# Two-block transformer kernel: order of the opening DMAs and of head 0's projections, and gate columns on GpSimd

## The reference, cut to what matters

```python
mod = silu(c) @ ada_w0 + ada_b0              # c: 1024, ada_w0: 1024 x 3072
shift, scale, gate = split(mod, 3)
h = rmsnorm(x, norm_g0) * (1 + scale) + shift
q, k, v, z = split(h @ w_in0, 4)             # w_in0: 1024 x 4096
q, k = rope(q), rope(k)                      # 8 heads, 2 components of 64 each
p = softmax(q0 k0) - lam * softmax(q1 k1)    # per head
o = rmsnorm(p @ v) * silu(z)
x = x + gate * (o @ w_out0)
```

## Time and profile before

| | us |
|---|---|
| median of 3 runs | 3085.14 |
| lowest and highest of them | 3079.88, 3085.21 |
| the profiled execution | 3082.07 |
| its span in the trace | 3080.3 |

### The profile page before, as it was taken

The page is one execution under the profiler, slowest core; times in us unless marked ns, Lnnn a source line. Parts: engine busy times, 40 slices in busy tenths (PEclk is TensorE's granted clock), DMA queues, the critical chain, the costliest instruction groups (busy, mean ns, idle before and its releaser), DMA issues.

```text
span 3080.3 us, 34996 instructions
## 1 busy us (share of the span) xinstructions
PE 2777.5 (90%) x13113; PEld 2176.5 (71%) x13113; DVE 1675.0 (54%) x2177; ACT 1307.7 (42%) x1842; POOL 0.2 (0%) x4
## 2 busy tenths in 40 slices
PE   4899999997889988898987789998689999999996
PEld 2677777775667766676766567666567878888775
DVE  5688888887453055555554635554644434334344
ACT  4567666665224133333332435565424313223232
POOL 0000000000000000000000000000000000000000
PEclk7999999998889999999999889999799999999998
DMA  7211111110211111121221310000211111111111
GB/s 257 98 39 43 48 48 44 45 34 27 89 34 45 50 56 47 50 67 49 67 61 41 106 41 21 28 15 14 82 41 41 44 51 46 50 48 40 49 42 68
DMA packets 215821, 166.96 MB, mean 54 GB/s; under 512 B 9562, under 2 KB 203058, under 8 KB 215730
## 3 DMA queue, kind: packets, MB, share of 16 engines
q1 hardware_dynamic: 215530, 165.68, 17.3%
q10 hardware_dynamic: 200, 0.06, 0.0%
HBM read 153.14 MB, written 12.58 MB: 54 GB/s over the span
## 4 chain that ended last, share of the span: by engine, by line
PE 79%; DVE 8%; ACT 5%; DVEq 2%; issue 2%; SPq 1%; DMA 1%; ACTq 0%
PE PS L516 19%; PE PS L518 18%; PE PS L517 18%; PE PS L1012 4%; PE PS L1666 3%; PE PS L985 2%; PE PS L999 2%; PE PS L989 1%; PE PS L1621 1%; PE PS L1656 1%; PE PS L2155 1%; PE PS L2168 1%; DVEq L1808 1%; PE PS L2179 1%; DVE rest L507 1%
## 5 line engine op out<-in xcount | busy, mean ns | idle before, releaser
L516 PE MATMUL PS<-h_high,w_high 128*128 128x512 f32 x2144 | 858.8, 401 | 59.8 <-DVE h_low L583 18.9
L517 PE MATMUL PS<-h_low,w_high 128*128 128x512 f32 x2144 | 844.7, 394 | 0.0
L518 PE MATMUL PS<-h_high,w_low 128*128 128x512 f32 x2144 | 844.6, 394 | 0.0
L516 PEld LDWEIGHTS PS<-h_high,w_high 128*128 128x128 f32 x2144 | 408.7, 191 | 159.6 <-issue 62.7
L518 PEld LDWEIGHTS PS<-h_high,w_low 128*128 128x128 f32 x2144 | 407.7, 190 | 87.1
L517 PEld LDWEIGHTS PS<-h_low,w_high 128*128 128x128 f32 x2144 | 408.8, 191 | 81.8 <-issue 0.5
L538 DVE TENSOR_TENSOR w_low<-raw_weights,w_high 128x1024 fp32r<-128x1024 f32 (+2 forms) x159 | 182.9, 1155 | 216.3 <-ACT w_high L533 215.5
L533 ACT ACTIVATE w_high<-raw_weights 128x1024 fp32r<-128x1024 f32 (+2 forms) x159 | 158.6, 1001 | 243.8 <-PE PS L518 233.1
L765 DVE SCALAR_TENSOR_TENSOR residual<-PS,rest,residual 128x512 f32 (+1 forms) x112 | 83.3, 750 | 244.2 <-PE PS L518 240.5
L1088 ACT ACTIVATE residual<-PS,rest 128x1024 f32<-128x1024 f32 x128 | 141.4, 1110 | 174.3 <-DVE rest L1217 174.3
L2717 DVE SCALAR_TENSOR_TENSOR gated<-rest,gated 128x1024 f32<-128x1024 f32 x44 | 56.6, 1286 | 255.0 <-ACT gated L2686 255.0
(11 more groups left out here) (307 smaller groups left out, 3972.5 us busy)
## 6 DMA issues: line engine op xcount, KB each, us to landing
raw_weights<-in_w_in SPq DMA_DIRECT2D x59, 512.0 KB, 4.1
activations<-in_w_ada SPq DMA_DIRECT2D x16, 1536.0 KB, 7.0
raw_weights<-in_w_up SPq DMA_DIRECT2D x44, 512.0 KB, 3.9
raw_weights<-in_w_out SPq DMA_DIRECT2D x24, 512.0 KB, 4.1
rest<-in_ada_w SPq DMA_DIRECT2D x16, 576.0 KB, 4.9
activations<-in_ada_w SPq DMA_DIRECT2D x8, 1024.0 KB, 13.7
x_kept<-residual SPq DMA_DIRECT2D x2, 4096.0 KB, 13.3
residual<-x_kept SPq DMA_DIRECT2D x2, 4096.0 KB, 13.5
```

What stands on the lines that cost most here:

```text
L516: e.matmul(out_, wh[:, k, :], xh[:, k, cols], start=first, stop=False)
L517: e.matmul(out_, wh[:, k, :], xl[:, k, cols], start=False, stop=False)
L518: return e.matmul(out_, wl[:, k, :], xh[:, k, cols], start=False, stop=last_k)
```

## The change

1. All nineteen vector pieces are sent from ScalarE's queue at the start; SyncE sends only the `lam` vectors after its large loads.
2. Head 0 projects queries and keys in phase A and z and values in phase B. `place` maps a chunk to its position and bank. ScalarE and VectorE do the queries and keys with their high and low parts first; z, values, head 1's first weight split and silu(z) follow.
3. The gate columns' products and sums move from VectorE to GpSimd, as 8 multiplications in place and 7 additions for each of two halves. It starts when norm 0 is done. TensorE's `mod_pe` for them comes behind chunks 6 and 7, and VectorE's `mod_out` between the low parts of queries and keys.
4. The second half of the shift: ScalarE's copy before tile 1 instead of tile 3, TensorE's columns behind the second contraction tile of phase A instead of ahead of it.

```diff
--- before.py
+++ after.py
@@ sync_small, sync_gates, scalar_loads
     def sync_small(e):
-        load_pieces(e, pieces[10:])
...
         for i in range(2):
-            e.dma_start(first_raw[i], w_cols("w_in0", (1 + i) * D, P)).then_inc(slot_full[2 + i], 16)
+            e.dma_start(first_raw[i], w_cols("w_in0", (3 - i) * D, P)).then_inc(slot_full[2 + i], 16)
...
     def scalar_loads(e):
-        load_pieces(e, pieces[:10])
+        load_pieces(e, pieces)
@@ tensor_setup
         shift_products(e, 1)
-        shift_columns(e, 1)
@@ the gate columns
-    def gate_products(e, i):
-        ada_products(e, 2 + i, gates[i], {0: (gate_ld[i], 48 if i else 16)})
+    def gpsimd_gates(e):
+
+        e.wait_ge(s["md_acc"], 2)
+        e.wait_ge(n0_ready[0], n0_ready[1] + NT)
+        for i in range(2):
+            x = gates[i]
+            e.wait_ge(gate_ld[i], 48 if i else 16)
+            for k in range(NT):
+                e.tensor_scalar(x[k], x[k], silu_c[:, k:k + 1], None, ALU.mult)
+            for k in range(1, NT):
+                e.drain()
+                last = e.tensor_tensor(x[0], x[0], x[k], ALU.add)
+            last.then_inc(s["md_acc"], 1)
@@ norm, scalar part
-                    if scalar_after is not None and t == 3:
+                    if scalar_after is not None and t == 1:
@@ diff_attention
+        FIRST_ORDER = [Q, Q + 1, Q + 2, Q + 3, 0, 1, V_AT, V_AT + 1]
+
+        def place(hh, c):
+
+            return FIRST_ORDER.index(c) if isinstance(hh, int) and hh == 0 else c
...
         def bank(hh, c):
-            return banks(c if isinstance(hh, int) and hh == 0 else PJ)
+            return banks(place(hh, c) if isinstance(hh, int) and hh == 0 else PJ)
...
         def sync(e):
             for i in range(2):
-                load_tile(e, 0, i)
+                e.dma_start(raw[i], w_cols("w_in0", COLUMNS[1 + i] * P, P)).then_inc(full[i], 16)
@@ pe_first
                     if k == NT - 1:
                         last.then_inc(pj, 1)
+                if k == 1:
+                    shift_columns(e, 1)
...
                 last.then_inc(pj, 1)
-                if c in (4, 6):
+                if c > 5:
                     e.wait_ge(pjA, 1)
-                    mod_pe(e, c // 2, 0, ada_acc, 4)
+                    mod_pe(e, c - 4, 0, gates[c - 6][0], 4)
@@ act_chunk
-            e.wait_ge(pj, 8 * hh + c + 1)
+            e.wait_ge(pj, 8 * hh + place(hh, c) + 1)
@@ diff_attention, scalar
-            for c in range(8):
+            for c in range(Q, V_AT):
                 act_chunk(e, 0, c)
-                if c == 5:
-                    act_split(e, 1, 0)
-            act_silu(e, 0)
 
             e.wait_ge(s["x_kept"], 16)
             act_query_high(e, 0, QUERIES)
             act_key_high(e, 0)
             act_key_copy(e, 0)
+            for c in (0, 1, V_AT, V_AT + 1):
+                act_chunk(e, 0, c)
+            act_split(e, 1, 0)
+            act_silu(e, 0)
@@ diff_attention, vector
-            for i in range(2):
-                gate_products(e, i)
-                for c in range(Q + 2 * i, Q + 2 * i + 2):
-                    dve_rope(e, 0, c)
-                mod_out(e, 2 + i, 16 + 4 * i, column["ada_b0"] + 16 + 4 * i, 0, 4)
-            dve_split(e, 1, 0)
+            for c in range(Q, V_AT):
+                dve_rope(e, 0, c)
             e.wait_ge(s["x_kept"], 16)
             dve_query_low(e, 0, QUERIES, 0)
+            for i in range(2):
+                mod_out(e, 2 + i, 16 + 4 * i, column["ada_b0"] + 16 + 4 * i, 0, 4)
             dve_key_low(e, 0)
+            dve_split(e, 1, 0)
@@ end of the program
+    @blk.gpsimd
+    def _(e):
+        gpsimd_gates(e)
```

## The result

The changed kernel is slower. Its median is 3101.04 us (3092.68 to 3103.08), beside 3085.14 us (3076.02 to 3087.78) for the kernel before on the same chip: ratio 1.0052, 95% interval 1.0038 to 1.0066. The forecast was 3075.4 us in a range of 3065 to 3088, so the time lies outside the range and the sign is the opposite of the one forecast. What came is rival 3, the slower side: GpSimd itself is slow at these instructions. The profiled execution took 3103.08 us with a span of 3101.3, 21.0 us above that of before.

What follows compares the result with a forecast made beforehand. TensorE (79% of the chain) was taken as the bound. Norm 0's end 86.0, GpSimd 29.8, contention 6.7 and 4.2 us put scores at 126.7, not 133.40: 3082.07 less 6.7 is 3075.4 us, range 3065 to 3088.

Steps and rivals of the forecast that it cites:

- rival 3: GpSimd itself slow at the gate sums: at 2.5 times VectorE's times, scores at 140.7 and 3089.4 us; chance 0.10.
- GpSimd alone, 29.8 us: Gate-column sums on GpSimd without contention: 14.9 us per half, 29.8 us for both, at 1.7 times VectorE's times.
- Norm 0's end, 86.0: Norm 0 was to end at 86.0 instead of 86.75, 0.7 us earlier; GpSimd's gate sums start then.
- Rival 4: Opening gives nothing, through held-up issues or `lam` vectors landing at 43: 3.9 us missing, time 3079.3 us; chance 0.05.
- The first term, 3.9 us from the opening: Opening: `lam` vectors land near 41.0, moving the lambda multiplication from 44.95 to 41.0, 3.9 us; bounds 2 to 5.
- The two new waits: Norm 0: high and low parts held behind the shift copies, 1.9 us, and VectorE waiting for `shift_columns`, 1.3 us.
- Phase A, first matmul at 66.8: TensorE ends `shift_products` at 66.8 and starts phase A then, instead of at 74.7.
- Contention, 6.7 us: VectorE's work beside GpSimd's gate sums delays their end by 6.7 us, the middle of bounds 0 and 13.5.
- From the last sum to the scores, 4.2 us: After GpSimd's last sum, `mod_pe`, `mod_out` and the key and last query low parts take 4.2 us before the scores.
- The claim that ScalarE and the queries are hidden: Before head 0's scores, query and key work and ScalarE's 7 us of later work cost nothing, covered by the gate-column wait.
- from 133.40 on all moves as one block: From head 0's first scores on, TensorE sets the pace and everything shifts together by the 6.7 us gained.
- rival 2: Only one of VectorE and GpSimd works at a time: 13.5 us added, scores at 133.5, 3082.2 us; chance 0.22.

Runs made afterwards that it cites:

- experiment 11: Changed kernel, but SyncE issues head 0's first weight columns only after the lambda product: 3096.04 us, ratio 1.0047 to the kernel before.
- 12: Kernel before with all vector pieces on ScalarE's queue and the first weight columns issued behind the lambda product: 3082.94 us, ratio 1.0005.
- experiment 1: Changed kernel with GpSimd's gate-column products and additions left out, so results are wrong: 3074.57 us, ratio 0.9974 to the kernel before.
- experiment 4: Changed kernel with GpSimd starting when its gate rows have landed, not after norm 0: 3075.74 us, ratio 0.9980 to the kernel before.
- experiment 6: Kernel before with all vector pieces and the four `lam` vectors sent from ScalarE's queue: 3063.99 us, ratio 0.9938.

## Why the prediction was wrong

It had the path right: the last `mod_pe` waits for GpSimd, `mod_out` waits for that, and the key low parts stand behind it. It had the sizes wrong. The scores were forecast at 126.7 and started at 144.82, 18.1 us later. By the prediction's own terms:

- **GpSimd alone, 29.8 us: +14.8.** This is the step that failed: the ratio of 1.7, taken from the memset, as the price of all of GpSimd's instructions. By the changed kernel's rows the undisturbed work is 16 multiplications of 1.56 us and 14 additions 1.40 us apart, 44.6 us. The ratio to VectorE's 17.5 us is 2.5, where I took 1.7 from a one-column memset, and the rival's condition for "slower" was 2.09. The ratio isn't even one number: 3.2 for the multiplication (1.56 / 0.49), 1.9 for the addition (1.28 / 0.69). At 1.7 the addition had been put at 1.17 us, not far off, but the multiplication at 0.83, half of what it took: 11.6 of the 14.8 us are the multiplications'. The memset writes one column and says nothing of the rate at 512. The mistake is less the value than the weight: a row of one column where the instruction has 512 can carry a bound, but not a chance of 0.10 for all ratios above 2.09. With r = 2.5 the prediction's rival 3 has the scores at 141 and the time at 3089 to 3090.
- **Norm 0's end, 86.0: +4.2.** `keep_x`, at 86.75 before, came at 90.05, and GpSimd started at 90.20. Rival 4 held too. The first term, 3.9 us from the opening (bounds 2 to 5), was 0.7. What failed in it is that the `lam` vectors are issued near 29 and land when the large loads do, near 41.0. The last of them was issued at 35.14 and landed 9.05 us later, at 44.19. With nothing issued behind them they still land 2.4 us later than forecast (43.4 in experiment 11 against 41.0), and 0.8 to 1.9 us more is due to a transfer that I didn't ask about (experiments 11 and 12). The first weight columns wait for the row statistics. These were ready at 51.9 in the kernel before, and are by 29.0 us in the changed one; so 1 MB that had left at 51.9 leaves at 35.8, right behind the `lam` rows, while the large loads still fill the DMA engines. I had moved ScalarE's work forward and put the row statistics at 30 to 35 us myself, and not looked at what they release on SyncE's queue. Of the 0.7 us nothing reached phase A. In the changed kernel TensorE idles for 20 us before the first `mod_pe`, which starts at 51.92 and takes 1.88 us; in the kernel before it started at 52.65, behind work, and took 1.07, so VectorE's `mod_out` stands at 53.83 beside 53.74. The two new waits that the prediction put into the norm, 1.9 and 1.3 us, were right: 1.69 and 1.38. One reading was off without entering the sum: VectorE's wait for the exponential was 22.8 us, not as long as TensorE's 27.2.
- **Phase A, first matmul at 66.8:** it came at 70.55, wholly because the opening gave nothing: `shift_products` stands at 65.55 with 5.06 us, as good as unmoved from the earlier trace rows. The move of `shift_columns` did what was said, from 74.7 to 70.55, 4.1 us. TensorE's wait before tile 1 was forecast at 1.0 us and was 0.84. In experiment 1, where phase B has no wait, the `mod_pe` behind its last chunk starts at 117.71 where 113.3 was forecast: the start's lateness and 0.7 us.
- **Contention, 6.7 us: -1.9.** GpSimd took 49.4 us (90.20 to 139.61) for 44.6, so 4.8 us, of bounds 0 and 13.5. The middle had been taken because nothing in the trace decided; that it came near is luck. VectorE paid too: the twelve rotations took 13.5 us instead of 8.3.
- **From the last sum to the scores, 4.2 us: +1.0.** It was 5.2, since `mod_pe` took 1.85 us at the lower clock instead of the 0.8 to 1.0 taken. The granted clock fell during TensorE's own wait: its mean is 0.63 from 126.60 to 139.70, and 0.50 from 139.7 to 145.

The four terms with a sign sum to 18.1 us; phase A's lateness is part of norm 0's. The claim that ScalarE and the queries are hidden held, and "from 133.40 on all moves as one block" held nearly. The trace is 11.4 us late at the scores and 13.4 at the end of head 0; those 2.0 us begin with TensorE's first matmuls behind the stall, whose pitch is 0.43 us until 150.3 where it was 0.23 before. Behind head 0 the profiled execution loses another 7.4 us in steps of about 3. The first scores don't decide them: experiment 11 has the same scores to 0.06 us, and is 13.6 us late at the end where the changed kernel is 20.8. What makes up the remaining 4.5 us between the shift at the scores (11.4) and that of the medians (15.9) isn't settled. Chance can be a good part of it, since the ratio's interval, 1.0038 to 1.0066, means 11.7 to 20.4 us, and the changed kernel's seven executions lie between 3092.68 and 3103.08, the profiled one being the slowest.

Full exclusion (rival 2) was wrong in size. By that rule, as the Trainium skill has it (SBUF — State Buffer, section Who interferes with whom), an instruction of VectorE with two SBUF inputs and one of GpSimd that reads SBUF shut each other out. The single instructions look like that: beside GpSimd's additions a rotation of 0.69 us takes up to 1.77, beside the norm a multiplication of 1.56 us takes up to 2.70 (experiment 4). GpSimd's very first, at 90.20 in the changed kernel, takes 3.57: it ends 1.5 us behind VectorE's two splits (89.94 to 92.29), as if it had begun with their end. But the first two rotation instructions, at 96.23 and 96.84 in the midst of GpSimd's multiplications, take 0.69 each, and the multiplication that runs beside the first of them (95.30 to 96.84) isn't stretched either. The third takes 1.03, and the sum is 4.8 us on GpSimd, not 13.5. So the trace agrees for some pairs and not for others.

On GpSimd's price the Trainium skill (GPSIMD Engine Reference, section Engine selection) says that a one-input operation on GpSimd is "roughly line-rate" and a two-input one about twice as slow as VectorE. The trace agrees on the addition (1.9) and contradicts it on the multiplication by a per-partition scalar, which is the slower of the two: 1.56 us, 3.2 times VectorE's.

## What to carry to other kernels

Before work is moved to an engine that the trace shows idle, its price has to come from an instruction of the same kind and size, and where there is none, the chance of "slow" must be as wide as the unknown ratio: here an idle engine took 2.5 times as long instruction by instruction, 3.6 times as long as the form of the work that it replaced, and became the bound with two stalls in series. No run put the second `mod_pe` and `mod_out` behind the first scores, which don't use the gate columns, so whether GpSimd could have been hidden that way isn't tested. When a wait is removed by sending some small transfers first, list all small transfers that the same engine chain still needs, and what the earlier engine will release: nine of thirteen rows early gave nothing, thirteen of thirteen gave 20.9 us at the scores. Work moved from VectorE to GpSimd came back in part as longer instructions on VectorE.

## What the runs showed of the hardware

- GpSimd on 128x512 fp32: multiplication by a per-partition scalar in place 1.56 us, addition 1.26 to 1.28 us, additions with a `drain` between them 1.40 us apart. An addition is cheaper than the multiplication with one tile operand.
- VectorE and GpSimd at work together slow single instructions of each other by up to 2.6 times (VectorE's 0.69 to 1.79 us, experiment 4; GpSimd's 1.56 to 3.57, changed kernel), but only in some pairings.
- Four small broadcast rows (32 KB each in SBUF) take 7.4 to 11.3 us from issue to landing while the DMA share is about 1, on SyncE's queue at 30 to 35 us (changed kernel) and on ScalarE's at 8 to 10 us (experiment 6) alike. Issued at 35.9 to 37.3 us, just before the share falls at 41, they took 5.5 to 5.8 (kernel before). What holds them isn't shown.
- Behind stalls of 5.83 and 12.50 us, and behind the 20 us without work before norm 0, the same eight matmuls of `mod_pe` took 1.84 to 1.88 us at a granted clock of 0.50 (1.2 GHz); with TensorE at work before them they took 0.95. In `shift_products` a start 0.78 us earlier didn't end earlier, since the rise to 1.00 (2.4 GHz) came 0.7 us later (experiment 11 beside the changed kernel).
